# Where the expert blocks' bias products stand in TensorE's order

## The chip, the cores and the metric

The kernel runs on one core of one Trainium2 chip. The metric is the device time of one execution in microseconds (us). The kernel before was timed in three runs: median 1827.28 us, lowest 1826.29 us, highest 1833.17 us.

## The reference, cut to what matters

The kernel computes one step of a one-layer decoder for 512 prompt tokens and 8 sequences of 8 sample tokens (576 tokens, width 1024): an input projection, two token mixers, an output projection, and a mixture of experts with 32 experts of which each token takes 4. The change lies in the mixture of experts. There the tokens are grouped by expert into blocks of up to 128 rows, and for each block the reference does:

```
xb = h_pad[tok]
gate = jnp.minimum(xb @ w_gate[e] + b_gate[e], SWIGLU_LIMIT)
up = jnp.clip(xb @ w_up[e] + b_up[e], -SWIGLU_LIMIT, SWIGLU_LIMIT)
return ((up + 1.0) * gate * jax.nn.sigmoid(SWIGLU_ALPHA * gate)) @ w_down[e] + b_down[e]
```

All three weights of an expert are 1024x1024 float32. The down bias is added elsewhere and isn't touched. The change is about where `b_gate[e]` and `b_up[e]` enter the sums.

## The kernel before, in words

The expert stage (`experts`) handles one block of 128 gathered rows after another; each block has its own expert. A weight matrix comes in four quarters of 1 MB each. SyncE (SP) issues their DMAs into a ring of 6 landing places; ScalarE (`high_part`, L2946) rounds a quarter to the high part; VectorE (`rest_part`, L3035) subtracts to get the low part; TensorE (`product`, L2842) multiplies with both parts. Rounded and low parts lie in rings of 4 places each. The semaphore `s_rest` counts quarters that are split, `s_used` quarters that TensorE has multiplied, so each ring's producer waits for the consumer.

One product is 4 quarters x 2 k-tiles x 6 = 48 matmuls of 128x128 with 512 columns, into two PSUM banks. For block k, TensorE's order in the loop (`step`, L2906) is:

1. `gate(k)` (L2853): waits for the split rows and for the reads of the gate and up banks of the block before; then four bias products, two for the gate banks and two for the up banks (`start_with_bias`, L2823, matmul at L2828); then the 48 matmuls of the gate product.
2. `turn_act(k)` (L2873): 8 transposes (L2850) of the activations of block k-1.
3. `up(k)` (L2862): 48 matmuls.
4. `turn_rows(k+1)` (L2865): 8 transposes of the gathered rows of the next block.
5. `down(k)` (L2879): 48 matmuls, the down product of block k-1.

A bias product multiplies a matrix of ones (3 rows x 128) with the bias in three bfloat16 parts (3 rows x 512), and opens the sum in its bank (`start=True`). The four of them read four different groups of 32 partitions: `bias_row(m, c)` is 64*m + 32*c, so the gate bias lies at rows 0 and 32, the up bias at rows 64 and 96. Each goes to its own bank.

SP's order for block k, with prev = k-1 (`step`, L2742): read the expert number, `biases(0, ...)` and `biases(1, ...)` (L2718, the small DMAs at L2724, two for the gate and two for the up bias), four quarters of gate weights, four of up weights, four of down weights of block prev (`quarters`, L2728; each DMA in `load_quarter`, L2620). The bias DMAs wait for `s_used` so that they don't overwrite a bias that TensorE still needs; each quarter waits for `s_rest`.

VectorE reads the gate banks into `gates` (`read_gate`, L3048) and the up banks into `ups` (`read_up`, L3054).

In the prologue TensorE does `turn_rows(0)`, reads four words of the block table (`used_blocks`), then `gate(0)`, `up(0)`, `turn_rows(1)`, a small product (`overflow`, 40 short matmuls at L2893), and then `step(1, 0)`. After the loop come the last turn of activations, without a bias, and the last down product.

Of the kernel before, what the change touches and what calls it, by code (L numbers as in the profile page):

```python
# [2594 lines left out]
def is_zero(n):  # L2595

    return isinstance(n, int) and n == 0
# [30 lines left out]
def experts(core):  # L2628
# [34 lines left out]
    GB, UB, DB, TB = 0, 2, 4, 6  # L2663
# [28 lines left out]
    def bias_row(m, c):  # L2692

        return 64 * m + 32 * c
# [17 lines left out]
    with nc.Block() as block:  # L2712
        @block.sync
        def _(sp):
            def expert(k):
                return sp.value_load(blocks[0:1, bass.ds(k, 1)], min_val=0, max_val=NE - 1)

            def biases(m, e, used):  # L2718

                if used is not None:  # L2720
                    sp.wait_ge(s_used, used)
                for c in range(2):
                    r0 = bias_row(m, c)
                    sp.dma_start(bias[r0:r0 + 3, :].rearrange("a (q n) -> a q n", q=2),  # L2724
                                 core.bias_d[bass.ds(e, 1), 2 * c:2 * c + 2, :, m, :].rearrange("e q a n -> (e a) q n")
                                 ).then_inc(s_bias[m], 16)

            def quarters(m, e, prev, c):  # L2728

                for q in range(4):  # L2730
                    sp.wait_ge(s_rest, 12 * prev + c + q + 9 - LANDING)
                    load_quarter(core, sp, e, m, q, (8 + c + q) % LANDING)

            e = expert(0)
            biases(0, e, None)
            biases(1, e, None)

            for q in range(2, 4):
                sp.wait_ge(s_rest, q - 1)
                load_quarter(core, sp, e, 1, q, q - 2)  # L2740

            def step(k, prev):  # L2742

                free = 1 if is_zero(prev) else 12 * prev
                e = expert(k)
                biases(0, e, free)
                biases(1, e, free)
                quarters(0, e, prev, 0)
                e = expert(k)
                quarters(1, e, prev, 4)  # L2750
                e = expert(prev)
                quarters(2, e, prev, 8)

            nb, nb1 = used_blocks(sp, 2)
            step(1, 0)
            with sp.Fori(2, nb) as k:
                step(k, k - 1)
            e = expert(nb1)
            quarters(2, e, nb1, 0)
            sp.wait_ge(s_yo, 16 * nb1)  # L2760
            for t in FINAL:
                t0, n = TILES[t]
                sp.dma_start(f[0:n, t, :], core.ffn_d[t0:t0 + n, :]).then_inc(s_f[t], 16)
            sp.wait_ge(s_xtp, nb)
            sp.dma_start(gfin, io["g_final"].unsqueeze(0).to_broadcast([P, D])).then_inc(s_gf, 16)
            for i, t in enumerate((FINAL[4], FINAL[0], FINAL[3], FINAL[1], FINAL[2])):
                t0, n = TILES[t]
                sp.wait_ge(s_oa if t in BY_ACT else s_o, i // 2 + 1)
                dst = io["out_0"][0, t0:t0 + n, :] if t < ST else io["out_1"].rearrange("b t d -> (b t) d")
                sp.dma_start(dst, f[0:n, t, :]).then_inc(s_out, 16)  # L2770
            sp.wait_ge(s_out, 16 * NT)
# [49 lines left out]
        @block.tensor  # L2821
        def _(pe):
            def start_with_bias(m, n, bank):  # L2823

                pe.wait_ge(s_bias[m], 32 * n)
                for c in range(2):
                    r0 = bias_row(m, c)
                    pe.matmul(ps[:, bank + c, :], ones[r0:r0 + 3, :], bias[r0:r0 + 3, :], start=True, stop=False)  # L2828

            def product(m, xs, bank, before):  # L2830

                for q in range(4):
                    j = 4 * m + q
                    pe.wait_ge(s_rest, before + q + 1)
                    for i in range(QK):
                        kt = QK * q + i
                        hi = [high[:, j % RING_Q, i, c * 512:(c + 1) * 512] for c in range(2)]
                        lo = [rest[:, j % RING_Q, i, c * 512:(c + 1) * 512] for c in range(2)]
                        terms = [(xs[0], hi[0], 0), (xs[0], hi[1], 1), (xs[0], lo[0], 0), (xs[0], lo[1], 1),
                                 (xs[1], hi[0], 0), (xs[1], hi[1], 1)]  # L2840
                        for x, wt, c in terms:
                            last = pe.matmul(ps[:, bank + c, :], x[:, kt * P:(kt + 1) * P].bitcast(F32R), wt.bitcast(F32R),  # L2842
                                             start=(m == 2 and kt == 0 and x is xs[0] and wt is hi[c]),
                                             stop=(kt == KT - 1 and x is xs[1]))
                    last.then_inc(s_used, 1)

            def turn(src, sem):
                v = src.rearrange("s (p k) -> s k p", k=KT)
                for kt in range(KT):
                    last = pe.transpose(ps[:, TB + kt // 4, (kt % 4) * P:(kt % 4 + 1) * P], v[:, kt, :], ident)  # L2850
                last.then_inc(sem, 1)

            def gate(k, before):  # L2853
                pe.wait_ge(s_xt, k + 1)
                if not is_zero(k):
                    pe.wait_ge(s_g, k)
                    pe.wait_ge(s_u, k)
                start_with_bias(0, k + 1, GB)
                start_with_bias(1, k + 1, UB)
                product(0, (xh, xl), GB, before)  # L2860

            def up(k, before):  # L2862
                product(1, (xh, xl), UB, before)

            def turn_rows(k, first=False):  # L2865
                pe.wait_ge(s_xg, 16 * (k + 1))
                if not first:
                    pe.wait_ge(s_at, k - 1)
                elif k == 1:
                    pe.wait_ge(s_xt, 1)  # L2870
                turn(xg, s_xtp)

            def turn_act(k):  # L2873

                pe.wait_ge(s_a, k)
                pe.wait_ge(s_xt, k + 1)
                turn(u, s_atp)

            def down(n, done, before):  # L2879

                pe.wait_ge(s_at, n)
                if is_zero(done):
                    pe.wait_ge(s_tab, 1)
                else:
                    pe.wait_ge(s_y, done)
                product(2, (ah, al), DB, before)

            def overflow():

                pe.wait_ge(s_over, 1)  # L2890
                for t, (t0, n) in enumerate(TILES):
                    for j in range(TOPK):
                        last = pe.matmul(ps[:, DB, 0:2 * OVER], core.at_row[0:n, t, j, :],  # L2893
                                         core.at_over[0:n, t, j].rearrange("p w k -> p (w k)"),
                                         start=(t == 0 and j == 0), stop=(t == NT - 1 and j == TOPK - 1))
                last.then_inc(s_ob, 1)

            pe.wait_ge(s_ones, 1)
            turn_rows(0, first=True)
            nb, nb1, nb2, _ = used_blocks(pe)  # L2900
            gate(0, 0)
            up(0, 4)
            turn_rows(1, first=True)
            overflow()

            def step(k, prev, last=False):  # L2906
                gate(k, first_of(prev))
                turn_act(k)
                up(k, first_of(prev) + 4)
                if not last:  # L2910
                    turn_rows(k + 1)
                down(k, prev, first_of(prev) + 8)

            step(1, 0)
            with pe.Fori(2, nb1) as k:
                step(k, k - 1)
            step(nb1, nb2, last=True)

            pe.wait_ge(s_a, nb)
            turn(u, s_atp)  # L2920
            down(nb, nb1, first_of(nb1))

            def last_rows(t, src):
                t0, n = TILES[t]
                for c in range(2):
                    last = pe.matmul(ps[0:n, BANK[t] + c, :], hot[:, t0:t0 + n], src[:, c * 512:(c + 1) * 512], start=True, stop=True)
                last.then_inc(s_last, 1)

            pe.wait_ge(s_hot, NT)
            pe.wait_ge(s_y, nb)  # L2930
            last_rows(ST, y)
            pe.wait_ge(s_yg, 1)
            for t in range(ST):
                if t == 3:
                    pe.wait_ge(s_read, 1)
                last_rows(t, yg)
# [266 lines left out]
```

## Time and profile before

| | us |
|---|---|
| median of 3 runs | 1827.28 |
| lowest, highest | 1826.29, 1833.17 |
| span of the profiled execution | 1826.6 |

The span is what the profiler recorded from first to last instruction of one execution; no other time of that execution is given. In it:

| | before |
|---|---|
| start of the expert stage (first transposes) | 651.21 us |
| one block in the loop (bias products to bias products) | 35.07 us |
| blocks | 32 |
| TensorE busy in the whole span | 1688.7 us, 92% |
| VectorE busy | 1435.0 us, 79% |
| ScalarE busy | 1105.6 us, 61% |

PE is TensorE's matmuls, PEld its weight loads, DVE VectorE, ACT ScalarE, POOL GpSimdE, SP SyncE. A line such as L2842 names the instruction's line in the kernel. In the chain of waits each piece is the time that the piece adds to the chain, from the end of what came before it to its own end.

### The profile page before, as it was taken

To read this page: it belongs to the slowest core of one execution; us is meant where nothing else is said; L and a number is where in the kernel's file an instruction comes from. 1 tells how busy PE (TensorE), PEld (TensorE's weight loads), DVE (VectorE), ACT (ScalarE), POOL (GpSimd) and SP (SyncE) were. 2 spreads that over 40 slices of the span, in tenths; PEclk is the share of its full clock that TensorE was granted. 3 is DMA by queue.
4 is the path that set the end of the run, shared out by engine and by line. 5 is a ranking of instruction groups with operands and counts; after the bars stand their busy time and mean duration, and the time that the engine had idled before them with its cause. 6 is when DMAs were issued, how large, how long until landed. Compare 5 with 4: busy or idle time off the path is not lost.

```text
span 1826.6 us, 26990 instructions
## 1 busy us (share of the span) xinstructions
PE 1688.7 (92%) x9012; PEld 1315.2 (72%) x9012; DVE 1435.0 (79%) x1353; ACT 1105.6 (61%) x1057; POOL 330.2 (18%) x310
## 2 busy tenths in 40 slices
PE   3999978789798779999999999999999999999995
PEld 2777666556554458888888888888888888888873
DVE  4422375477434879999999999999999999999996
ACT  4221244355333457777777777777777777777772
POOL 0000102200011011222312312322221231232110
PEclk9999879799899779999999999999999999999997
DMA  9454474410136378999999999999999999999973
GB/s 347 158 188 168 82 213 151 146 64 1 48 118 177 145 289 325 374 378 373 370 382 375 371 376 377 374 376 375 378 373 380 378 370 382 381 373 370 389 283 123
DMA packets 114598, 516.08 MB, mean 283 GB/s; under 512 B 25870, under 2 KB 47710, under 8 KB 62058
## 3 DMA queue, kind: packets, MB, share of 16 engines
q1 hardware_dynamic: 101082, 483.48, 70.5%
q0 software_dynamic: 12800, 29.45, 5.8%
q10 hardware_dynamic: 656, 2.36, 0.3%
q8 instruction: 36, 0.59, 0.1%
q14 instruction: 24, 0.20, 0.0%
HBM read 502.75 MB, written 31.09 MB: 292 GB/s over the span
## 4 chain that ended last, share of the span: by engine, by line
PE 61%; DVE 2%; ACT 1%; DMA 1%; issue 0%; DVEq 0%; POOL 0%; ACTq 0%; POOLq 0%
PE banks L2842 57%; PE banks L2850 3%; PE banks L2828 1%; DMA ffn_rows<-weighed,block_rows 0%; DVE arena L3113 0%; DVE arena L3112 0%; ACT sigmoids L3014 0%; DVE split L3035 0%; PE banks L2893 0%; ACT split L2946 0%; DMA arena<-ffn_rows 0%; DVE arena L3131 0%; DVEq L2709 0%; ACT final_stat L3015 0%; ACT L3020 0%
## 5 line engine op out<-in xcount | busy, mean ns | idle before, releaser
L2842 PE MATMUL banks<-split 128*128 128x512 f32 x4608 | 1079.4, 393 | 6.9 <-DVE split L3039 5.8
L2842 PEld LDWEIGHTS banks<-split 128*128 128x128 f32 x4608 | 862.8, 189 | 192.6 <-issue 13.2
L3035 DVE TENSOR_TENSOR split<-expert_buffers,split 128x2048 fp32r<-128x2048 f32 x384 | 864.7, 2284 | 42.3 <-ACT split L2946 40.6
L2946 ACT ACTIVATE split<-expert_buffers 128x2048 fp32r<-128x2048 f32 x384 | 732.9, 1918 | 219.2 <-PE banks L2842 215.1
L2781 POOL TENSOR_TENSOR wait_taken<-routing 128x1 f32<-128x1 f32 x62 | 76.0, 1226 | 811.4 <-PE banks L2850 464.4
L2804 POOL DMA_INDIRECT ffn_rows<-weighed,block_rows x31 | 107.7, 3476 | 4.8 <-issue 4.8
L526 PE MATMUL banks<-w_in_high,hT_high 128*128 128x476 f32 x192 | 75.7, 394 | 4.2 <-DVE hT_low L413 4.2
L439 DVE COPY arena<-banks 128x476 f32<-128x476 f32 x12 | 7.8, 654 | 91.1 <-PE banks L526 91.0
L3039 DVE TENSOR_TENSOR split<-banks,split 128x1024 fp32r<-128x1024 f32 x64 | 77.7, 1215 | 0.7 <-ACT split L2949 0.7
L526 PE MATMUL banks<-w_in_high,hT_low 128*128 128x476 f32 x192 | 73.4, 382 | 0.0
L2949 ACT ACTIVATE split<-banks 128x1024 fp32r<-128x1024 f32 x64 | 64.4, 1006 | 4.3 <-PE banks L2850 4.3
L2971 ACT ACTIVATE weighed<-banks,block_weights 128x1024 f32<-128x1024 f32 x32 | 35.7, 1117 | 46.0 <-PE banks L2842 46.0
L526 PE MATMUL banks<-w_in_low,hT_high 128*128 128x476 f32 x160 | 60.5, 378 | 0.0
L1743 ACT ACTIVATE arena<-banks 128x512 f32<-128x512 f32 (+1 forms) x45 | 24.5, 586 | 58.0 <-PE banks L2007 19.3
L1413 ACT ACTIVATE arena<-banks,arena 128x128 f32<-128x128 f32 (+3 forms) x64 | 33.2, 526 | 38.7 <-DVE arena L1455 38.6
L526 PEld LDWEIGHTS banks<-w_in_high,hT_high 128*128 128x128 f32 x192 | 36.7, 191 | 21.7 <-issue 16.7
L2963 ACT ACTIVATE sigmoids<-gates 128x1024 f32<-128x1024 f32 x32 | 34.0, 1063 | 25.9 <-DVE gates L3048 25.9
L2786 POOL TENSOR_TENSOR routing<-routing 128x1 int32<-128x1 int32 x31 | 40.6, 1308 | 16.2 <-issue 8.6
L2850 PEld LDWEIGHTS banks<-routing 128*128 128x128 f32 x256 | 33.9, 192 | 9.4 <-DVE bias_ones L3030 6.9
L526 PEld LDWEIGHTS banks<-w_in_high,hT_low 128*128 128x128 f32 x192 | 36.6, 191 | 5.7
L687 POOL MEMSET arena<- 128x2560 f32 x1 | 2.2, 2235 | 212.7 <-POOLq L122 212.7
L2850 PE MATMUL banks<-routing 128*128 128x128 f32 x256 | 34.5, 279 | 6.1 <-DVE bias_ones L3030 6.1
(399 smaller groups left out, 1741.8 us busy)
## 6 DMA issues: line engine op xcount, KB each, us to landing
expert_buffers<-in_w_gate SPq DMA_DIRECT2D x128, 1024.0 KB, 8.5
expert_buffers<-in_w_up SPq DMA_DIRECT2D x128, 1024.0 KB, 6.4
expert_buffers<-in_w_down SPq DMA_DIRECT2D x128, 1024.0 KB, 8.8
arena<-in_w_ada SPq DMA_DIRECT2D x16, 1024.0 KB, 4.8
w_in_landing<-in_w_in SPq DMA_DIRECT2D x5, 1904.0 KB, 16.8
arena<-in_w_ada SPq DMA_DIRECT2D x4, 2048.0 KB, 19.7
arena<-in_x_prompt SPq DMA_DIRECT2D x8, 512.0 KB, 7.2
arena<-in_cache_cmp POOLq DMA_DIRECT2D x32, 128.0 KB, 3.4
```

The costliest lines, as they stand in the source:

```text
L526: last = pe.matmul(ps[0:n, 4 + t, 0:CW], h[:, kt, t0:t0 + n].bitcast(F32R), w.bitcast(F32R), start=(kt == 0 and j == 0), stop=(kt == KT - ...
L2781: pool.tensor_tensor(sums[s_sum.index(sem)], one, one, ALU.add).then_inc(sem, 1)
L2786: pool.tensor_tensor(tokens, core.row_of[:, bass.ds(k, 1)], none, ALU.add).then_inc(s_tok, 1)
L2804: pool.indirect_dma_start(core.ffn_d, bass.IndirectOffsetOnAxis(ap=row_out.bitcast(U32), axis=0), y, None, bounds_check=NTOK - 1, oob_is_e ...
L2842: last = pe.matmul(ps[:, bank + c, :], x[:, kt * P:(kt + 1) * P].bitcast(F32R), wt.bitcast(F32R), start=(m == 2 and kt == 0 and x is xs[0] ...
L2850: last = pe.transpose(ps[:, TB + kt // 4, (kt % 4) * P:(kt % 4 + 1) * P], v[:, kt, :], ident)
L2946: act.activation(high[:, j % RING_Q].bitcast(F32R), v, ACT.Copy).then_inc(s_high, 1)
L2949: act.activation(dst.bitcast(F32R), ps[:, TB:TB + 2, :].rearrange("p b n -> p (b n)"), ACT.Copy).then_inc(sem, 1)
L2963: act.activation(s, g, ACT.Sigmoid, scale=ALPHA).then_inc(s_sig, 1)
L2971: act.activation(y, ps[:, DB:DB + 2, :].rearrange("p b n -> p (b n)"), ACT.Copy, scale=weight_out).then_inc(s_y, 1)
L3035: dve.tensor_tensor(rest[:, j % RING_Q].bitcast(F32R), v, high[:, j % RING_Q], ALU.subtract).then_inc(s_rest, 1)
L3039: dve.tensor_tensor(lo.bitcast(F32R), ps[:, TB:TB + 2, :].rearrange("p b n -> p (b n)"), hi, ALU.subtract).then_inc(out, 1)
```

## The change

The two gate bias products move from the head of `gate(k)` to the end of `turn_rows(k)`, that is, behind the turn of the rows, one product earlier. The two up bias products move to the end of `turn_act(k)`, directly ahead of the up product. The waits on the reads of the banks (`s_g`, `s_u`) move with them. On SP, the DMAs of the up bias move behind the first two gate quarters, and wait for one more quarter to be used.

```diff
-            def quarters(m, e, prev, c):
-
-                for q in range(4):
+            def quarters(m, e, prev, c, some=range(4)):
+
+                for q in some:
                     sp.wait_ge(s_rest, 12 * prev + c + q + 9 - LANDING)
                     load_quarter(core, sp, e, m, q, (8 + c + q) % LANDING)
...
             def step(k, prev):
 
-                free = 1 if is_zero(prev) else 12 * prev
                 e = expert(k)
-                biases(0, e, free)
-                biases(1, e, free)
-                quarters(0, e, prev, 0)
+                biases(0, e, 1 if is_zero(prev) else 12 * prev)
+                quarters(0, e, prev, 0, range(2))
+                biases(1, e, 5 if is_zero(prev) else 12 * prev + 1)
+                quarters(0, e, prev, 0, range(2, 4))
...
             def gate(k, before):
                 pe.wait_ge(s_xt, k + 1)
-                if not is_zero(k):
-                    pe.wait_ge(s_g, k)
-                    pe.wait_ge(s_u, k)
-                start_with_bias(0, k + 1, GB)
-                start_with_bias(1, k + 1, UB)
                 product(0, (xh, xl), GB, before)
...
                 turn(xg, s_xtp)
+                if not is_zero(k):
+                    pe.wait_ge(s_g, k)
+                start_with_bias(0, k + 1, GB)
 
             def turn_act(k):
 
                 pe.wait_ge(s_a, k)
                 pe.wait_ge(s_xt, k + 1)
                 turn(u, s_atp)
+                pe.wait_ge(s_u, k)
+                start_with_bias(1, k + 1, UB)
...
             turn_rows(0, first=True)
+            start_with_bias(1, 1, UB)
             nb, nb1, nb2, _ = used_blocks(pe)
             gate(0, 0)
```

## Rows read from the trace of the kernel before

**Rows 1.** The page: span, then busy us (share) and count of an engine.

```profile
span 1826.6 us, 26990 instructions
...
PE 1688.7 (92%) x9012; PEld 1315.2 (72%) x9012; DVE 1435.0 (79%) x1353; ACT 1105.6 (61%) x1057; POOL 330.2 (18%) x310
```

**Rows 2.** Busy time by stage: window and length, engines' busy us, PEclk, DMA share, GB/s.

```profile
1200.00:1400.00 200.00, 200.00 (x936) 164.29 (x935) 193.13 (x104) 151.49 (x91) 53.92 (x42) 1.00 0.99 375
```

**Rows 3.** The chain of waits, 1190 to 1300 us: start, us, what.

```profile
1205.02 10.89 PE banks L2842 x48
1215.91 0.33 PE banks L2828 x4
1216.24 11.16 PE banks L2842 x48
1227.40 0.89 PE banks L2850 x8
1228.28 10.92 PE banks L2842 x48
1239.20 0.89 PE banks L2850 x8
1240.09 10.89 PE banks L2842 x48
1250.98 0.33 PE banks L2828 x4
```

**Rows 4.** PE in order of time: start, us, engine, line, operation, tiles, shape, count.

```profile
1215.85 0.40 PE L2828 MATMUL banks<-block_biases,bias_ones 3*128 3x512 bf16 x4
...
1754.14 22.05 PE L2842 MATMUL banks<-split 128*128 128x512 f32 x96
```

**Rows 5.** Tile block_biases: duration ns min/median/max, then PEld's idle time, times.

```profile
L2828 PE MATMUL banks<-block_biases,bias_ones x128: 384/385/605, 656.3 to 1742.0; 3*128 3x512 bf16 x128
...
  issue: 10.6, 30
```

**Rows 6.** PEld in order of time, around bias products, then around a turn.

```profile
1215.84 0.10 PEld L2828 LDWEIGHTS banks<-block_biases,bias_ones 3*128 3x128 bf16 x4 [0.35 <-issue]
1216.17 2.86 PEld L2842 LDWEIGHTS banks<-split 128*128 128x128 f32 x13 [0.23 <-issue]
...
1227.00 1.09 PEld L2850 LDWEIGHTS banks<-routing,ups 128*128 128x128 f32 x8
1228.01 1.00 PEld L2842 LDWEIGHTS banks<-split 128*128 128x128 f32 x5
```

**Rows 7.** DVE in order of time: the reads of the up and gate banks.

```profile
1205.60 1.22 DVE L3054 TENSOR_SCALAR ups<-banks 128x1024 f32<-128x1024 f32 x1
...
1228.86 1.22 DVE L3048 TENSOR_SCALAR gates<-banks 128x1024 f32<-128x1024 f32 x1
```

**Rows 8.** SP's DMA issues in order of time, the loop, then the prologue.

```profile
1228.02 1.62 SPq L2724 DMA_DIRECT2D block_biases<-bias_parts  x4
1229.88 9.04 SPq L2620 DMA_DIRECT2D expert_buffers<-in_w_gate  x4
...
652.18 1.65 SPq L2724 DMA_DIRECT2D block_biases<-bias_parts  x4
...
664.31 5.62 SPq L2620 DMA_DIRECT2D expert_buffers<-in_w_gate  x4
```

**Rows 9.** DMA issues of 1228 to 1263 us: KB each, us to landing.

```profile
expert_buffers<-in_w_down SPq DMA_DIRECT2D x4, 1024.0 KB, 10.2
```

**Rows 10.** PE in order of time in the prologue.

```profile
656.34 0.61 PE L2828 MATMUL banks<-block_biases,bias_ones 3*128 3x512 bf16 x4 [3.15 <-DVE split L3039]
656.88 21.80 PE L2842 MATMUL banks<-split 128*128 128x512 f32 x84
...
688.44 12.84 PE L2842 MATMUL banks<-split 128*128 128x512 f32 x48
```

**Rows 11.** ACT in order of time in the prologue.

```profile
684.63 3.70 ACT L2946 ACTIVATE split<-expert_buffers 128x2048 fp32r<-128x2048 f32 x2
```

## The prediction

> **What bounds the kernel now.** I read the page first: TensorE (PE) is busy 92% of a span of 1826.6 us, VectorE 79% [rows 1]. An average says little about the place of the change, so next the windows of the expert stage: in 200 us in its middle PE is busy for all 200.00 us at the full granted clock, VectorE for 193.13 us, and the DMA engines for a share of 0.99 [rows 2]. Three resources are close together, and the question is which of them waits for no other. The chain of waits answers it: through two whole stretches it stays on PE and consists of nothing but products of 48 matmuls, turns of 8 transposes, and the bias products [rows 3]. No piece of waiting for DMA, VectorE or ScalarE stands between them. One period is the distance of two bias groups: 1250.98 - 1215.91 = 35.07 us, and the pieces fill it: 0.33 + 11.16 + 0.89 + 10.92 + 0.89 + 10.89 = 35.08. So in the loop the time is the length of PE's own stream. Whatever adds to this stream costs its full length; whatever is only moved within it costs nothing, unless its price depends on its neighbours.
>
> **What the bias products cost now.** Per block there are four (128 in the trace, 32 blocks). Their median length is 385 ns [rows 5], four one after the other would be 1.54 us; but the group of four takes 0.40 us [rows 4], hardly more than one of them. So the four run side by side: they read four different groups of 32 partitions and write four banks. The group's price is not the length of the matmuls summed but one passage, plus what it costs to enter and leave. Entering and leaving show in the weight loads: around a turn they follow without a gap, but ahead of the bias group PEld is idle for 0.35 us and behind it for another 0.23 us [rows 6]; the first of these recurs, 10.6 us in 30 groups, 0.35 each [rows 5]. In the chain the group is 0.33 us, and the product behind it takes 11.16 us where the products behind turns take 10.92 and 10.89, mean 10.905 [rows 3]. The price of one group is thus 0.33 + (11.16 - 10.905) = 0.585 us. What a boundary between two products costs without a bias group shows at the end of the stage: two products on end take 22.05 us in order of time [rows 4], against 2 x 10.905 = 21.81 by the chain, and that view counts the last matmul's overlapping tail too. So it costs at most 0.24 us and probably about nothing.
>
> The Trainium skill has the rule for this, "TensorEngine Tiling (Array Packing)", section Tiling Modes, Key Properties: tiles work independently of each other, and "Mode switching requires drain". The trace agrees with both: four matmuls in the time of one, and a gap in the weight loads at either side. By that rule two groups would cost two entries and two exits wherever they stand, which is the way this change goes; if instead the price went by the number of matmuls, the change would be free.
>
> **The change part by part.**
>
> *Removed:* one group of four from the head of each gate product. That gives back 0.585 us per block.
>
> *Added:* two groups of two, one behind each turn. No row shows a pair. From above: it costs no more than the group of four, 0.585 us, since a pair has the same length as its longest member. From below: if the price went by the matmuls, half, 0.29 us; and below that nothing, if the 0.35 and 0.23 us of idle weight loads were hidden by the turn's short transposes. A turn shows the weight loads without a gap [rows 6], so it has no stall of its own in which a pair could hide. The nearest row is the group of four itself: a member takes as long alone as beside three others, and both idle pieces belong to entry and exit. A part of the 0.255 us lost in the product behind could belong to the gate product itself (its loads' gap is 0.23, which leaves some 0.03). I take 0.33 + 0.23 = 0.56 us for a pair. Net per block: 2 x 0.56 - 0.585 = 0.535 us. It counts for the 31 blocks after the first: 31 x 0.535 = 16.6 us. With 0.585 it is 31 x 0.585 = 18.1; with 0.29, nothing; with a hidden pair, down to -0.585 x 31 = -18.1.
>
> *Moved waits on PE.* The gate pair behind `turn_rows` needs the gate banks read: VectorE reads them from 1228.86 for 1.22 us [rows 7], and the turn ends at about 1240.09 [rows 3], 10 us later. The up pair behind `turn_act` needs the up banks read: begun at 1205.60, needed at 1228.28 [rows 7, 3], 21 us. Both are long over. Behind either waiting pair stands a whole product, and with it everything else, but neither waits.
>
> *The gate bias DMA.* It's now needed one product earlier. It is issued at 1228.02 [rows 8], two of the four issues of 0.4 us each, so all of it by 1228.85; TensorE needs it at 1240.09, 11.2 us later. A transfer of 3 KB stands in the queue behind down quarters of 1 MB whose landing took 10.2 us in this stretch [rows 9]. It follows the last of them, so it should land near 10 us from issue: a margin of about 1 us from the row. That is the narrowest place of the change; I take it as held, cost nothing, and price the other case below.
>
> *SP's queue.* The up bias DMAs (0.8 us of issuing) move behind the second gate quarter. Ahead of them the first gate quarter goes out 0.8 us earlier, if its buffer is free. Behind them stand the gate quarters three and four, then all the rest. In the loop the added wait (one more quarter used) is implied by the wait of the third quarter: a quarter can be split only when the one four places back has been used. The issues of the four gate quarters stretch over 9.04 us [rows 8], so SP waits for buffers there and the 0.8 us fall into that wait. Cost nothing; the bounds are 0 and a delay of 0.8 us in a queue whose quarters land ahead of need.
>
> *Prologue.* First, the biases of block 0: PE waits 3.15 us for the split rows, and the group of 0.61 us stood behind this wait [rows 10]. Now it stands ahead of it and can hide, a gain of up to 0.6 us; but the four reads of the block table on PE now come behind it, and behind the landing of biases issued up to 653.83 [rows 8]. With a landing as slow as in the loop that could be 3 us late. Bounds -0.6 and +3; since the queue is nearly empty then, I take 0. Second, the second block's third gate quarter was issued within 664.31 to 669.93 [rows 8]; now it waits until the first up quarter of block 0 is used. 84 matmuls, seven quarters, end at 678.68 [rows 10]; two quarters back at 2.73 us each (a quarter of 10.905) is 673.2. With the bias issues it goes out at about 674.1 and is needed by ScalarE at 684.63 [rows 11], 10.5 us later, against 10.2 us for a full queue. It is hidden, just. Third, the gate product of block 1 takes 12.84 us instead of 11.1 [rows 10], part of it at the half clock behind the short matmuls; that stretch may fall otherwise, 1.7 us either way. I take 0.
>
> **Sum.** Against the profiled execution's span of 1826.6 us: +16.6 gives 1843.2. The span stands 0.7 us under the median of the runs, 1827.28; carried over to the median, 1843.9 us, rounded 1844. That is +0.9%. I count about 0.5% (9 us) as what this kernel's measurement can tell from no change, so the line lies at 1836.4.
>
> **The rivals.**
>
> *Pairs at half price or partly hidden (no change).* If a pair behind a turn costs 0.29 us, for instance because the turn's transposes are over sooner than the long matmuls of a product, the net is 0 and the time 1827. The point from which the verdict turns is 9.1/31 = 0.29 us net, a pair at 0.44 us: below it the change isn't measurable. For it: no row shows the entry from a transpose. Against it: the idle of the weight loads lies on both sides, and the exit is into the same product as before. Chance 0.13.
>
> *Pairs wholly hidden (faster).* The group of four goes and nothing comes: 31 x -0.585 = -18, time 1809. For it: a turn's weight loads and matmuls are half of the array's work only. Against: the weight loads run back to back through a turn [rows 6]. Chance 0.04, with anything under -0.5%.
>
> *The gate bias lands late (slower still).* Place: the wait at the pair behind `turn_rows`. It decides from a landing of 11.2 us after issue. A landing of 12.2 us, 2 us above the row's 10.2, would stall PE for 1 us in each of 30 blocks: 1844 + 30 = 1874 us. For it: the DMA engines are at 0.99 [rows 2] and the margin is narrow. Against: longer blocks relax the queue, and only two small transfers stand behind the down quarters. Chance 0.05.
>
> **How the numbers follow.** The forecast case has 0.78: pairs between 0.44 and 0.6 us, prologue between -2 and +3, which gives 1836 to 1849. Slower by over 0.5%: 0.78 + 0.05 = 0.83. Within 0.5%: 0.13. Faster: 0.04. The range reaches from 1835 to 1850; it leaves out the late landing and both cases below.
>
> **What would show it.** In the trace after: (1) two groups x2 at L2828 in each period, each about 0.40 us long in order of time and 0.33 in the chain, with idle weight loads ahead of and behind each; (2) the gate product down from 11.16 to about 10.9, the up product and the down product up from 10.9 to about 11.15; (3) the period 35.6 instead of 35.07; (4) PE still without a piece of waiting in the chain; VectorE's and the DMA's shares in the loop down by about 1.5%. I am wrong if the pairs are much shorter than 0.33 us in the chain, if the products behind them keep 10.9, or if a wait for a DMA stands ahead of the pair behind the rows' turn.

## The result, and the profile after

The changed kernel takes 1846.41 us (median of 4 runs, 1845.82 to 1849.56) against 1826.78 us (4 runs, 1825.92 to 1833.17): a ratio of 1.0101, 95% interval 1.0083 to 1.0120. It's slower by 19.6 us, with 15 to 22 us in the interval. The profiled execution has a span of 1844.1 us and took 1845.82 us.

The chain of waits of the changed kernel, in the middle of the loop (start, us, what), answers to [rows 3]:

```profile
1214.15 0.89 PE banks L2850 x8
1215.03 0.32 PE banks L2828 x2
1215.35 22.00 PE banks L2842 x96
1237.35 0.89 PE banks L2850 x8
1238.24 0.32 PE banks L2828 x2
1238.56 11.12 PE banks L2842 x48
...
1250.57 0.32 PE banks L2828 x2
```

Between two gate pairs lie 1250.57 - 1215.03 = 35.54 us, against 35.07 before: +0.47 us. The chain still consists of PE's stream alone. Each block now has two groups x2 of 0.32 us, and each is about as long as the one group x4 was (0.33). The gate product no longer shows by itself, since nothing separates it from the down product ahead of it: the two together take 22.00 us.

The members of a pair last as long as those of the group of four did, 385 ns in the median (tile block_biases, changed kernel). In the windows of 1200 to 1400 us (as [rows 2]) VectorE is busy for 190.21 us instead of 193.13, 1.5% less as forecast; the DMA engines' share falls from 0.99 to 0.98, and what they moved from 375 to 373 GB/s:

```profile
L2828 PE MATMUL banks<-block_biases,bias_ones x128: 384/385/604, 657.2 to 1771.3; 3*128 3x512 bf16 x128
...
1200.00:1400.00 200.00, 200.00 (x927) 163.94 (x927) 190.21 (x103) 150.03 (x91) 36.03 (x39) 1.00 0.98 373
```

PE in order of time, changed kernel: the first transposes, the first block's two bias groups, the first product, the first turn of activations, and the last one:

```profile
654.15 1.97 PE L2850 MATMUL banks<-routing 128*128 128x128 f32 x8 [6.12 <-DVE bias_ones L3031]
657.15 0.61 PE L2828 MATMUL banks<-block_biases,bias_ones 3*128 3x512 bf16 x2 [1.03 <-DMA block_biases<-bias_parts]
657.92 0.60 PE L2828 MATMUL banks<-block_biases,bias_ones 3*128 3x512 bf16 x2 [0.16 <-DMA block_biases<-bias_parts]
660.87 4.36 PE L2842 MATMUL banks<-split 128*128 128x512 f32 x12 [2.34 <-issue]
...
704.09 1.05 PE L2850 MATMUL banks<-routing,ups 128*128 128x128 f32 x8
...
1793.51 1.05 PE L2850 MATMUL banks<-routing,ups 128*128 128x128 f32 x8
```

The same landmarks of the kernel before are 651.21, 656.88, 701.12 and 1776.03 us, the latter two in these rows of its PE in order of time:

```profile
701.12 1.05 PE L2850 MATMUL banks<-routing,ups 128*128 128x128 f32 x8
...
1776.03 1.05 PE L2850 MATMUL banks<-routing,ups 128*128 128x128 f32 x8
```

This divides the 17.5 us between the two spans:

| stretch | before | after | difference |
|---|---|---|---|
| start to the first transposes | 651.21 | 654.15 | +2.94 |
| to the turn of the activations in block 1 | 49.91 | 49.94 | +0.03 |
| loop, to the last turn | 1074.91 | 1089.42 | +14.51 |
| from there to the end | 50.57 | 50.59 | +0.02 |

The 14.5 us are the change: 30 periods longer by 0.47 us, and one up pair of 0.52 us in the last block, where no group of four was taken away. The code ahead of the first transposes is the same in both kernels, and in the profiled executions of the ten kernels of this study that differ only behind it this stretch took 646.17 to 656.02 us; its 2.94 us here are one draw from that spread. The second stretch spreads too: the kernel with only SyncE's part of the change (below) has the same order on TensorE as the kernel before, and took 48.62 us there instead of 49.91, with the gate product of block 1 at 11.22 instead of 12.84 us. The granted clock of 690 to 695 us was 1.00 in the one and 0.71 in the other. So the +0.03 says no more than that nothing large happened there. The loop hardly spreads: 1074.88 us with SyncE's part alone, and again 1089.42 us in the changed kernel with the block table read first.

The waits of the loop (690 to 1740 us; engine, line, waited for: us in total, times, longest us) hold no wait of PE for the bias DMAs, and the idle time of PEld behind a group, called issue, comes 59 times where it came 29 times:

```profile
PEld banks L2842 <- issue: 13.4, 59, 0.2
```

### The profile page after: what moved, and what is told of

Read it like the earlier page. It is cut to its first block, busy times and chain, and to the rows that moved or that the text cites. A ratio compares the mean times of both kernels' runs of the same rounds, so it can differ in the third digit from the quotient of the medians.

```text
span 1844.1 us, 27021 instructions
## 1 busy us (share of the span) xinstructions
PE 1697.7 (92%) x9012; PEld 1321.1 (72%) x9012; DVE 1437.8 (78%) x1353; ACT 1105.1 (60%) x1057; POOL 264.0 (14%) x310
## 4 chain that ended last, share of the span: by engine, by line
PE 60%; DVE 2%; issue 1%; ACT 1%; DMA 1%; DVEq 0%; POOL 0%; ACTq 0%; POOLq 0%
PE banks L2842 55%; PE banks L2850 3%; PE banks L2828 1%; DMA ffn_rows<-weighed,block_rows 0%; DVE arena L3114 0%; DVE arena L3113 0%; ACT sigmoids L3015 0%; DVE split L3036 0%; PE banks L2893 0%; ACT split L2947 0%; DMA arena<-ffn_rows 0%; DVE arena L3132 0%; DVEq L2709 0%; ACT final_stat L3016 0%; ACT L3021 0%
## 5 line engine op out<-in xcount | busy, mean ns | idle before, releaser
L2781 POOL TENSOR_TENSOR wait_taken<-routing 128x1 f32<-128x1 f32 x62 | 60.0, 967 | 890.6 <-PE banks L2850 525.9
L2804 POOL DMA_INDIRECT ffn_rows<-weighed,block_rows x31 | 53.7, 1732 | 4.8 <-issue 4.8
L2786 POOL TENSOR_TENSOR routing<-routing 128x1 int32<-128x1 int32 x31 | 42.3, 1364 | 17.5 <-DMA routing<-h_rows,routing 8.9
L3063 DVE TENSOR_TENSOR ups<-ups,sigmoids 128x1024 f32<-128x1024 f32 x32 | 39.3, 1227 | 1.1
```

What stands on the lines that cost most here:

```text
L2781: pool.tensor_tensor(sums[s_sum.index(sem)], one, one, ALU.add).then_inc(sem, 1)
L2786: pool.tensor_tensor(tokens, core.row_of[:, bass.ds(k, 1)], none, ALU.add).then_inc(s_tok, 1)
L2804: pool.indirect_dma_start(core.ffn_d, bass.IndirectOffsetOnAxis(ap=row_out.bitcast(U32), axis=0), y, None, bounds_check=NTOK - 1, oob_is_e ...
L3063: dve.tensor_tensor(u, u, s, ALU.mult).then_inc(s_a, 1)
```

## The experiments

Each is an edit of the kernel before or of the changed kernel, and the fences show its main part. "Period" is the time from one group to the same group a block later in the chain of waits. Where nothing else is said, the rows of a kernel show that chain.

### What a group costs: taken away

```diff
-                for c in range(2):
-                    r0 = bias_row(m, c)
-                    pe.matmul(ps[:, bank + c, :], ones[r0:r0 + 3, :], bias[r0:r0 + 3, :], start=True, stop=False)
...
-  start=(m == 2 and kt == 0 and x is xs[0] and wt is hi[c]),
+  start=(kt == 0 and x is xs[0] and wt is hi[c]),
```

> The kernel before without the gate and up bias products of the expert blocks (their part of the sum is left out; the bias DMAs stay, the first product of a sum opens it). My theory, a price of 0.585 us for the one group of four: the period falls from 35.07 to 34.49 us, the time by 31 x 0.585 = 18 us to about 1809. Rival 1, the weight of the group is its entry into the product only (0.33 in the chain, the slower product behind it being the gate product's own): period 34.74, time -10 us. Rival 2, the DMA engines at a share of 0.99 become the bound: 35.07 x 0.99 = 34.7 us, time -11 us at most, with pieces of DMA or ScalarE in the chain of waits.

Measured: 1809.83 us, ratio 0.9894 (0.9877 to 0.9910) to the kernel before at 1828.07.

```profile
1218.06 0.89 PE banks L2847 x8
1218.95 10.92 PE banks L2839 x48
1229.87 0.89 PE banks L2847 x8
1230.76 21.79 PE banks L2839 x96
1252.54 0.89 PE banks L2847 x8
```

The period is 1252.54 - 1218.06 = 34.48 us, 0.59 under 35.07: the price of the group of four is what the prediction read from the chain. The rival of 0.33 us would give 34.74. The DMA engines, at a share of 0.99 before, didn't become the bound, and these rows give the clean lengths: 10.92 us for the up product behind its turn, 21.79 us for down and gate on end. Since the down product alone takes 10.89, a gate product without a group ahead takes 10.90, and a boundary between two products costs nothing, as the prediction took it.

By the landmarks, the loop (from the turn of the activations in block 1 to the last turn) is 17.80 us shorter than before.

### Is it the shape of the tile? All 128 rows

Each bias product uses 128 rows, with zeros outside its three. VectorE sets up the zeros and ones once, ahead of the first block (not shown).

```diff
-                    r0 = bias_row(m, c)
-                    pe.matmul(ps[:, bank + c, :], ones[r0:r0 + 3, :], bias[r0:r0 + 3, :], start=True, stop=False)
+                    i = 2 * m + c
+                    pe.matmul(ps[:, bank + c, :], ones[:, i * P:(i + 1) * P], bias[:, :], start=True, stop=False)
```

> The kernel before with each of the four bias products over all 128 rows (zeros outside of the three bias rows), so that TensorE never changes the tile shape. My theory (entry and exit of a small tile shape cost, members run side by side): no idle weight loads around the group, four products one after the other at the pace of the stream, 4 x 0.227 = 0.91 us instead of 0.585, net +0.32 x 31 = +10 us, 1837; the product behind the group takes 10.9 us. Rival, the gaps come from the change of the data type (bfloat16 among float32): the gaps stay and the members no longer overlap, 0.585 + 3 x 0.227 = 1.27 us, net +0.68 x 31 = +21 us, 1848.

Measured: 1838.47 us, ratio 1.0057 (1.0040 to 1.0074).

```profile
1211.07 10.89 PE banks L2844 x48
1221.97 0.07 issue
1222.04 0.81 PE banks L2830 x3
1222.85 10.94 PE banks L2844 x48
...
1257.38 0.07 issue
```

From the end of the down product to the end of the gate product there are 0.07 + 0.81 + 10.94 = 11.82 us, that is 0.92 over a product of 10.90: four matmuls at the pace of the stream (0.91), with no entry and no exit. The period is 35.41. The operands are still bfloat16 among float32, so the data type isn't what costs; the small tile shape is. The chain shows x3 since the trace has records of 96 of these products beside 128 weight loads: one of each four is missing, so the 0.07 of issue needn't be idle time, and only the sum can be read. The small shape is still the better bargain for four (0.59 against 0.92). A pair over 128 rows would cost 2 x 0.227 = 0.45 us, an estimate from this pace that no run tested; a pair in the small shape costs 0.52.

PEld in order of time in this kernel shows a gap ahead of the group too, though the four cost no more than their pace (0.92 against 0.91):

```profile
1221.81 0.55 PEld L2830 LDWEIGHTS banks<-block_biases,bias_ones 128*128 128x128 bf16 x4 [0.26 <-issue]
```

So the gap in the weight loads ahead of a group isn't itself the price of the entry.

### Number or place: split without a turn

```diff
                 start_with_bias(0, k + 1, GB)
-                start_with_bias(1, k + 1, UB)
-                product(0, (xh, xl), GB, before)
+                product(0, (xh, xl), GB, before, lambda: start_with_bias(1, k + 1, UB))
```

The function passed in is called behind the first quarter of the product. SyncE's wait for the up bias of block 1 is one quarter later, to fit.

> The kernel before with the group split in two and not behind a turn: the gate pair at the head of the gate product, the up pair behind its first quarter. My theory, a price for each group wherever it stands: two groups x2 per block, period +0.5 to +0.585, time +15 to +18 us, about 1843, as the change. Rival, the price goes by the number of products (a pair at half price): period unchanged, time 1827. Rival, it is the neighbourhood of the turn that makes pairs dear: here +0, only the change +18.

Measured: 1848.55 us, ratio 1.0112 (1.0095 to 1.0129), at least the whole loss of the change with nothing behind a turn.

```profile
1216.34 10.89 PE banks L2842 x48
1227.23 0.32 PE banks L2828 x2
1227.56 2.99 PE banks L2842 x12
1230.54 0.32 PE banks L2828 x2
1230.86 8.44 PE banks L2842 x36
...
1262.89 0.32 PE banks L2828 x2
```

The period is 35.66. The gate product with both pairs takes 0.32 + 2.99 + 0.32 + 8.44 = 12.07 us, 1.17 over 10.90: twice 0.585, the full price of a group for each pair. In the loop this kernel is 17.40 us longer than the kernel before by the landmarks. That is somewhat more than expected (a period of up to +0.585, 15 to 18 us). The price goes by the number of groups; two products in one cost as much as four.

### Each half of the change alone

Only the gate pair moved (the up pair stands at the head of the gate product):

```diff
 # in turn_act (the call for block 0 goes from the prologue too)
-                pe.wait_ge(s_u, k)
-                start_with_bias(1, k + 1, UB)
 # in gate
+                if not is_zero(k):
+                    pe.wait_ge(s_u, k)
+                start_with_bias(1, k + 1, UB)
                 product(0, (xh, xl), GB, before)
```

> The changed kernel with the up pair put back at the head of the gate product: only the gate pair stands behind the turn of the rows. Theory (number of groups): still two groups per block, period 35.5 to 35.6, time +15 to +18 us over before, 1843 to 1846, like the whole change. Rival (each moved pair adds its own cost): half of the change, +8 us, 1835.

Measured: 1847.51 us, ratio 1.0091 (1.0064 to 1.0118) to 1829.51. Only the up pair moved is the mirror image (the gate pair at the head of the gate product):

> The changed kernel with the gate pair put back at the head of the gate product: only the up pair stands behind the turn of the activations. Theory (number of groups): two groups per block, period 35.5 to 35.65, time +15 to +18 us over before. Rival (each moved pair adds its own cost): +8 us, 1835. In this kernel both pairs' exits lie ahead of a product, so it may be a few tenths of a us per block over the whole change, in which only the up product and the down product are preceded by one.

Measured: 1845.71 us, ratio 1.0093 (1.0066 to 1.0120). The chain of the kernel with the gate pair moved:

```profile
1217.24 0.32 PE banks L2828 x2
1217.56 11.11 PE banks L2842 x48
1228.67 0.32 PE banks L2828 x2
1228.99 11.16 PE banks L2842 x48
...
1252.84 0.32 PE banks L2828 x2
```

and of the one with the up pair moved:

```profile
1224.43 0.32 PE banks L2828 x2
1224.75 11.16 PE banks L2842 x48
1235.90 0.89 PE banks L2850 x8
1236.79 0.32 PE banks L2828 x2
1237.11 11.12 PE banks L2842 x48
...
1260.02 0.32 PE banks L2828 x2
```

The periods are 35.60 and 35.59 us. Either half alone costs as much as the whole, even 0.05 us more; the halves don't add. (The few tenths more that the second expectation allowed for came to 0.05.) What costs is the step from one group to two.

### SyncE's part, and the prologue

Only SyncE's part of the change, on the kernel before:

```diff
-                biases(0, e, free)
-                biases(1, e, free)
-                quarters(0, e, prev, 0)
+                biases(0, e, 1 if is_zero(prev) else 12 * prev)
+                quarters(0, e, prev, 0, range(2))
+                biases(1, e, 5 if is_zero(prev) else 12 * prev + 1)
+                quarters(0, e, prev, 0, range(2, 4))
```

> The kernel before with only SyncE's part of the change: the up bias DMAs behind the second gate quarter, with their later wait. Theory: nothing, 1827 within 2 us, period 35.07, since SyncE waits for buffers there and the third quarter of the prologue goes out late but in time. Rival: the delayed gate quarter of the prologue holds TensorE back by 1 to 3 us once, 1828 to 1830, seen between the first product and the first block of the loop.

Measured: 1828.64 us, ratio 0.9999 (0.9987 to 1.0012), and the loop takes 1074.88 us against 1074.91 by the landmarks. It costs nothing. The changed kernel with the block table's reads ahead of the first biases:

```diff
-            turn_rows(0, first=True)
-            start_with_bias(1, 1, UB)
+            pe.wait_ge(s_xg, 16)
+            turn(xg, s_xtp)
             nb, nb1, nb2, _ = used_blocks(pe)
+            start_with_bias(0, 1, GB)
+            start_with_bias(1, 1, UB)
```

> The changed kernel with the four reads of the block table ahead of the first block's bias products, as in the kernel before. In the changed kernel the first product starts 6.72 us after the first transposes (before: 5.67), behind 1.63 us of issue in the chain. Theory: the reads of the table behind the landing of the biases cost this: the first product starts 5.1 to 5.7 us after the transposes. For the whole: ScalarE and VectorE are the chain in block 0, and in the changed kernel the distance from the first transposes to the second turn of the rows was 31.4 us as before, so a gain of 0 to 1 us, 1845 to 1846. Rival: the whole 1.0 to 1.6 us comes back.

Measured: 1846.87 us, ratio 1.0101 (1.0080 to 1.0123). PE in order of time:

```profile
646.17 1.97 PE L2850 MATMUL banks<-routing 128*128 128x128 f32 x8 [6.06 <-DVE bias_ones L3033]
...
651.29 5.06 PE L2842 MATMUL banks<-split 128*128 128x512 f32 x11 [0.78 <-DVE split L3042]
```

The first product starts 5.12 us after the first transposes (changed kernel 6.72), so the reads were the delay; but the median stays where it was. From the first transposes to the second turn of the rows there are 31.27 us here, 31.34 in the changed kernel and 31.42 in the kernel before: by then block 0 has waited for ScalarE and VectorE, and the head start is gone.

### One group, next to a turn

The four products can share a group beside a turn, if the gate bias closes its sum instead of opening it. SyncE issues all four bias DMAs behind the first two gate quarters (not shown):

```diff
+            def both_biases(n):
+                for m, bank in ((1, UB), (0, GB)):
+                    pe.wait_ge(s_bias[m], 32 * n)
+                    for c in range(2):
+                        r0 = bias_row(m, c)
+                        last = pe.matmul(ps[:, bank + c, :], ones[r0:r0 + 3, :], bias[r0:r0 + 3, :], start=(m == 1), stop=(m == 0))
+                last.then_inc(s_gated, 1)
...
                 turn(u, s_atp)
+                pe.wait_ge(s_u, k)
+                both_biases(k + 1)
...
             def read_gate(k, used):
-                dve.wait_ge(s_used, used)
+                dve.wait_ge(s_gated, k + 1)
```

> All four in one group, behind the turn of the activations: the up bias opens its sum, the gate bias closes the gate sum that was finished ahead of the turn (VectorE reads the gate banks only after it). One group per block as before, at the place of the change. My theory: the place is worth what a group behind a turn costs in the changed kernel, 0.32 + (11.12 - 10.90) = 0.54 us against 0.585, so the period falls by 0.045 and the time by 1.4 us to 1825.5. Rival, a group behind a turn costs more than between products: then a part of the change's +17 comes from the place and this kernel is slower than before, by some 5 us or more.

> The kernel with all four in one group behind the turn of the activations, again, for a narrower interval. Its trace had a period of 35.01 us against 35.07, so by the trace the time is 0.06 x 31 = 1.9 us under the kernel before, 1825.5; the rival is no difference. With runs that spread by 7 us ahead of the expert stage the interval may not tell them apart.

Measured: 1825.83 us, ratio 0.9991 (0.9977 to 1.0005) to 1828.07, and again 1825.82 us, ratio 0.9985 (0.9973 to 0.9998) to 1829.33.

```profile
1230.07 0.89 PE banks L2854 x8
1230.96 0.33 PE banks L2831 x4
1231.29 11.12 PE banks L2846 x48
...
1265.97 0.33 PE banks L2831 x4
```

The period is 35.01 us, the group costs 0.33 + (11.12 - 10.92) = 0.53. So the place at a turn is cheaper by 0.06 us, not dearer. With the group moved ahead of the turn, at the end of the gate product:

```diff
                 product(0, (xh, xl), GB, before)
+                if not is_zero(k):
+                    pe.wait_ge(s_u, k)
+                both_biases(k + 1)
```

> As the kernel with all four in one group behind the turn of the activations, but the group ahead of that turn: the exit is into short transposes. Theory 1, the exit costs one weight load that isn't hidden (0.11 us) and a slower start of the product, 0.20 us in all in the kernel with the group behind the turn; ahead of transposes, whose pace is that of a weight load, at most 0.11 of it stays: group 0.33 + 0.1 = 0.43 to 0.48 us, period 34.90 to 34.95, 4 to 5 us under the kernel before, 1823. Theory 2, the cost is the same at every place: period 35.01 to 35.07, 1825.5 to 1827.

Measured: 1824.81 us, ratio 0.9985 (0.9973 to 0.9996).

```profile
1225.41 0.33 PE banks L2831 x4
1225.74 1.09 PE banks L2854 x8
1226.83 10.93 PE banks L2846 x48
...
1260.42 0.33 PE banks L2831 x4
```

The turn behind the group takes 1.09 us instead of 0.89: the exit costs its 0.20 us there too. My first theory, a cheaper exit into transposes, falls; the period is 35.01 again. These two kernels are the fastest that compute everything, 0.15% ahead of the kernel before, and their intervals nearly touch 1. The shorter period accounts for 31 x 0.06 = 1.9 us of it, 0.1%; for the rest no source was looked for.

## Why the prediction was right, point by point

**The bound.** PE's stream fills the loop, and everything added to it costs its length: shown from both sides, -0.59 us a block where the group is missing gave -18 us, +0.59 for a pair in the middle of a product gave +20 us. The loop alone gives, by the landmarks, -17.80 and +17.40 us, and +14.51 us for the change.

**The price of the group of four, 0.585.** Measured 0.59. **The price of a pair, taken as 0.56.** The up pair costs 0.32 + (11.12 - 10.92) = 0.52, the gate pair 0.32 + (22.00 - 21.79) = 0.53. The mechanism held, and that a pair's members take as long as those of four, for which no row of before was evidence, held too (385 ns). The term was 0.03 to 0.04 too high for each, since I had only the group between two products to read, and that one is the dearest place. Net per block: 0.52 + 0.53 - 0.59 = 0.46 instead of 0.535, and the loop 14.5 instead of 16.6 us.

**"No wait of PE" and the gate bias DMA.** Held: no piece of DMA stands in the chain. How wide its margin of "about 1 us" really was, none of the shown rows tells; it wasn't squeezed.

**The evidence from the weight loads.** I read the idle 0.35 us of PEld ahead of the group as the entry's cost. That reading doesn't hold. PEld of the changed kernel in order of time, behind a turn:

```profile
1213.76 1.08 PEld L2850 LDWEIGHTS banks<-routing 128*128 128x128 f32 x8
1214.96 0.09 PEld L2828 LDWEIGHTS banks<-block_biases,bias_ones 3*128 3x128 bf16 x2
1215.28 21.64 PEld L2842 LDWEIGHTS banks<-split 128*128 128x128 f32 x96 [0.23 <-issue]
```

Behind transposes there's no idle time ahead of the pair, and it costs 0.32 in the chain all the same; with 128 rows there is idle time and nothing is lost. The gap behind (0.23) does go with the exit: with 128 rows the view lists none behind the group. So of the two gaps that the prediction took as signs of entry and exit, only the one behind the group is one. The price itself came from the chain, and so it held.

**SyncE and the prologue.** Both taken at 0: SyncE's part measured 0.9999, the prologue +0.03 us to the first turn of activations, in a stretch that differs by 1.3 us between two executions with the same order on TensorE. The hidden bias group was no gain, and the reads of the table, which I had bounded at +3, delayed the first product by 1.05 us, but block 0 gave that back. The stated reason for the zero, a nearly empty queue, was incomplete: PE did wait for the two landings.

**The total.** 1844 forecast, 1846.41 measured. From the loop the profile accounts for 14.5 of the 19.6 us between the medians. The interval of the ratio begins at 15 us. Of the 5 us that the loop doesn't hold, 2.9 lie ahead of the expert stage in the profiled pair, in a stretch that spreads by 10 us among the profiled executions. And the four runs of the kernel before came out low: its 49 runs in the rounds of the experiments have a median of 1828.85 us, against which the change costs 17.6 us. That the remaining 3 us hold nothing of the change is argued, not shown. So the mechanism was right, but the closeness of the total is in part luck: a loop term 2.1 us too large stands against a measured remainder that the prediction had at nothing.

One bound of the prediction is added up wrongly: pairs at 0.44 us and a prologue of -2 us give 1834, not 1836. The measured time lies far from it.

**The rivals.** Half price for a pair (0.29): refuted by the split inside the product. Pairs hidden by the turn: refuted, they are 0.06 to 0.07 us cheaper there and no more. The late bias: didn't happen.

## What to carry to other kernels

Products with few rows that run side by side on different partition groups cost one passage and an exit, two of them as much as four here: keep them in one group. If two sums can't be opened at the same time, let one group close the first and open the second; a bias may come anywhere in its sum. Where an engine's stream fills the chain without a gap, count the switches that an edit adds to it before asking what it may hide.

## What the runs showed of the hardware that I had not expected

- Two products of 3 rows take as long as four, 0.32 against 0.33 us in the chain, and the exit costs 0.20 to 0.27 us whether products or transposes follow. Groups of one and three weren't tried. Between or inside products it's 0.26 to 0.27, next to a turn 0.20 to 0.22; why, stays open.
- An idle gap of the weight loads ahead of a group (0.26 us) can go with nothing lost (0.92 us for four products over 128 rows, 0.91 by the pace of the stream), and no gap with the passage's full 0.32 us. It isn't a measure of what a switch costs.
- With PE's period shortened to 34.48 us the core moved 381 GB/s, over the 375 of [rows 2], without a wait: a share of 0.99 of the DMA engines wasn't yet the limit.

The windows of the kernel without bias products, for the last point (as [rows 2]):

```profile
1200.00:1400.00 200.00, 200.00 (x927) 167.08 (x926) 195.32 (x105) 154.30 (x94) 51.17 (x38) 1.00 0.99 381
```
